# First expert's rows by products, its second matrix loaded earlier, routing's scratch moved, side projection spread over the experts

## What is computed

```python
# hier_moe, cut
g_gate, g_idx = top_k(softmax(xf @ w_rg), 1)            # one of 4 groups
e_w, e_i = top_k(softmax(e_logits of that group), 2)    # two of its 8 experts
hdn = silu(xb @ w1[e]) * (xb @ w3[e])                   # xb: the rows that chose expert e
out[rows] += (hdn @ w2[e]) * weight
# side projection, cut
h = h + rms_norm(p @ w_ple, g_ple) * sigmoid(rms_norm(h, g_plg) @ w_plg)
```

## Time and profile before

| | us |
|---|---|
| median of three runs | 1856.92 |
| lowest and highest of them | 1851.44, 1857.51 |
| the profiled execution's own time | 1853.95 |
| its span, first to last instruction | 1852.2 |

### The profile page before, as it was taken

One profiled execution on the slowest core, in us unless ns is written; L12 is line 12 of the kernel. 1 busy time (PEld: TensorE's weight loads), 2 busy tenths in 40 slices (PEclk: granted clock), 3 DMA queues, 4 the chain that ended last, 5 costly groups with the idle time before them and its releaser, 6 DMA issues. The chain is left out here.

```text
span 1852.2 us, 24687 instructions
## 1 busy us (share of the span) xinstructions
PE 1762.2 (95%) x9926; PEld 970.2 (52%) x9926; DVE 748.6 (40%) x1472; ACT 545.0 (29%) x1110; POOL 153.7 (8%) x194
## 2 busy tenths in 40 slices
PE   8999988989889899999899999999999999999998
PEld 3333455455444444555464444577645544566663
DVE  2244477142511121433223225577524328365642
ACT  2111477123101111333224112455412232344420
POOL 0310000001111110111100014000000003000000
PEclk9999999999999999999999999999999999999999
DMA  7664877448999999999970232000200012000001
GB/s 274 227 219 169 114 153 67 162 166 347 419 418 416 416 417 417 420 416 418 397 294 2 90 103 79 1 2 1 84 23 35 23 63 68 24 1 2 1 24 45
DMA packets 92194, 324.85 MB, mean 175 GB/s; under 512 B 12313, under 2 KB 28825, under 8 KB 65073
## 3 DMA queue, kind: packets, MB, share of 16 engines
q1 hardware_dynamic: 78224, 302.55, 45.1%
q10 hardware_dynamic: 8656, 12.32, 1.9%
q0 software_dynamic: 5200, 8.41, 1.2%
HBM read 317.58 MB, written 14.30 MB: 179 GB/s over the span
## 5 line engine op out<-in xcount | busy, mean ns | idle before, releaser
L1089 PE MATMUL mix_ps<-arena 128*64 128x256 f32 x2048 | 238.6, 386 | 9.1 <-DMA arena<-in_w 4.9
L2175 PE MATMUL tail_ps<-arena 128*128 128x512 f32 x504 | 220.1, 593 | 0.8 <-DMA arena<-in_w_plg 0.8
L1089 PEld LDWEIGHTS mix_ps<-arena 128*64 128x64 f32 x2048 | 145.3, 138 | 95.8 <-issue 23.7
L977 PE MATMUL mix_ps<-arena,side 128*128 128x512 f32 x384 | 174.1, 606 | 0.6 <-DMA arena<-in_w_in 0.6
L484 DVE TENSOR_REDUCE tail_small<-tail_ps 128x1 f32<-128x768 f32 x128 | 116.6, 953 | 123.4 <-PE tail_ps L351 77.5
L2175 PEld LDWEIGHTS tail_ps<-arena 128*128 128x128 f32 x504 | 95.0, 190 | 115.0 <-issue 114.5
L1101 PE MATMUL mix_ps<-arena 128*64 128x512 f32 x512 | 118.6, 606 | 22.1 <-DMA arena<-in_w 22.1
L977 PEld LDWEIGHTS mix_ps<-arena,side 128*128 128x128 f32 x384 | 71.8, 193 | 101.1 <-issue 82.9
L2175 PE MATMUL tail_ps<-arena,side 128*128 128x512 f32 (+2 forms) x320 | 119.6, 534 | 0.0
L575 ACT ACTIVATE arena<-tail_ps,tail_small 128x768 f32<-128x768 f32 x128 | 113.7, 898 | 3.7 <-DVE tail_small L484 3.7
L370 PE MATMUL tail_ps<-first,arena 128*128 128x128 f32 x768 | 98.5, 279 | 0.6 <-ACT arena L575 0.6
(11 more groups left out here) (392 smaller groups left out, 2339.5 us busy)
## 6 DMA issues: line engine op xcount, KB each, us to landing
arena<-in_w SPq DMA_DIRECT2D x96, 2048.0 KB, 21.2
arena<-in_l_w_mod SPq DMA_DIRECT2D x16, 1024.0 KB, 5.1
arena<-in_l_w_in SPq DMA_DIRECT2D x16, 1024.0 KB, 7.0
arena<-in_w_in SPq DMA_DIRECT2D x12, 1024.0 KB, 9.1
arena<-in_l_w_mod SPq DMA_DIRECT2D x16, 512.0 KB, 4.7
residual<-bias_blocks SPq DMA_DIRECT2D x32, 224.0 KB, 12.9
arena<-in_l_w_in ACTq DMA_DIRECT2D x12, 512.0 KB, 11.0
arena<-in_l_w_out SPq DMA_DIRECT2D x6, 1024.0 KB, 5.2
```

What stands on the lines that cost most here:

```text
L977: last = pe.matmul(ps[:, u % 4], oT[:, k, t * P:(t + 1) * P], weights.slot(W_IN[n, k // 4], 4, 512)[:, k % 4], start=(k == 0), stop=(k == ...
L1089: last = pe.matmul(out[h * CAP:(h + 1) * CAP, 0:H2], x, wb[:, k, h * H2:(h + 1) * H2], start=(k == 0), stop=(k == DK - 1))
L2175: last = pe.matmul(out, lhs(k), rhs(k), start=(k == 0), stop=(k == K - 1))
```

## The change

Four edits. (1) Routing's scratch leaves slot 4 for parts of `work` and `base`, and SyncE issues w2 of expert 0 ahead of its wait for `out_mm`, with no wait for `listed`. (2) Expert 0's rows are no longer gathered by DMA. VectorE makes `taken_0`, a 128x64 matrix for each row tile that has a row's factor `rs_h` in the column of its slot, TensorE multiplies it with `hx` (8 products into bank 1, `listed` = 1), and ScalarE copies the result to `xg[:, 0]`. `list_slots` comes behind the turning of these rows, GpSimd starts with `gather(1)`, and `listed` is 2 when the lists are done. (3) VectorE writes `index[:, 1]` and `gate_w` behind `take_x(0)` and `index[:, 0]`. (4) Side projection units 4 to 7 move into the experts: unit 4 behind expert 0's w3 product, units 5 to 7 behind `second(0)` in the loop's e = 1; their copies on ScalarE move too (unit 4 behind expert 0's Silu, 5 to 7 behind `outputs(0)`). SyncE's wait for `side_ev` = 8 stays where it was.

```diff
-    r_at = [2 * 4096]
+    r_in, r_at = (work[:, 4096:6144], base[:, late + CT * D:late + CT * D + 2592]), [0, 0]
...
+    taken_0, factor_0 = routing(XT, CAP), routing(XT)
...
+            expert(0, "w2")
             sp.wait_ge(s["out_mm"], 8)
             expert(1, "w1")
             expert(1, "w3")
-            sp.wait_ge(s["listed"], 1)
-            expert(0, "w2")
...
-            beside(2)
-
+            pe.wait_ge(s["hot"], 1)
+            for t in range(XT):
+                for h in range(2):
+                    last = pe.matmul(ps[h * CAP:(h + 1) * CAP, 1], taken_0[:, t], hx[:, t, h * 512:(h + 1) * 512], start=(t == 0), stop=(t == XT - 1))
+            last.then_inc(s["listed"], 1)
...
-            list_slots(4, hot, told, 3 * N_EXPERTS, s["hot"], s["listed"])
-            beside(3)
...
-            turn_rows(xg[:, 0], s["got"][0], 16, s["xg_turned"])
+            turn_rows(xg[:, 0], s["xn_done"], XT + 1, s["xg_turned"])
+            list_slots(4, hot, told, 3 * N_EXPERTS, s["hot"], 1, s["listed"])
...
+                if e == 0:
+                    beside(2, (0,))
...
                 if e == 1:
+                    beside(2, (1,))
+                    beside(3)
                     pe.wait_ge(s["side_ev"], 2 * XT)
...
+            for u in range(4):
+                beside(u)
+            act.wait_ge(s["listed"], 1)
+            act.activation(xg[:, 0], ps[:, 1], ACT.Copy).then_inc(s["xn_done"], 1)
...
+                if e == 0:
+                    beside(4)
...
+                if e == 1:
+                    for u in (5, 6, 7):
+                        beside(u)
...
+            dve.tensor_tensor(factor_0, A_all[:, :, 0], rs_h, ALU.mult)
+            dve.wait_ge(s["ranked"], 1)
+            chain(dve.tensor_tensor(taken_0, m["count"][:, 0:CAP].unsqueeze(1).to_broadcast([P, XT, CAP]),
+                                    ps[:, 4, 0:XT * N_EXPERTS].rearrange("p (t e) -> p t e", t=XT)[:, :, 0:1].to_broadcast([P, XT, CAP]), ALU.is_equal))
+            dve.tensor_tensor(taken_0, taken_0, factor_0.unsqueeze(2).to_broadcast([P, XT, CAP]), ALU.mult).then_inc(s["hot"], 1)
...
-            for e in range(2):
-                gather(e)
+
+            gather(1)
```

More of the change, by code:

```diff
@@ L690, in first_layer @@
     experts_over, trips_over, current = small_i[0:1, 100:100 + OVER + 1], small_i[0:1, 118:119], view(small_i, 120, 2)
-    r_at = [2 * 4096]
+    r_in, r_at = (work[:, 4096:6144], base[:, late + CT * D:late + CT * D + 2592]), [0, 0]
     def routing(*dims):
         n = math.prod(dims)
-        r_at[0] += n
-        assert r_at[0] <= 3 * 4096
-        return view(proj_w, r_at[0] - n, *dims)
+        z = 0 if r_at[0] + n <= 2048 else 1
+        r_at[z] += n
+        assert r_at[1] <= 2592
+        return view(r_in[z], r_at[z] - n, *dims)
     wr = routing(DK, N_GROUPS + N_EXPERTS)
@@ L1036, in _, with beside @@
             pe.wait_ge(s["side_in"], 16)
-            def beside(t):
-                for cc in range(2):
+            def beside(t, parts=(0, 1)):
+                for cc in parts:
                     u = 2 * t + cc
@@ L1052, in _, with list_slots @@
             pe.matmul(ps[:, 4, 256:256 + N_EXPERTS], m["ones"], A_sum[:, XT], start=True, stop=True).then_inc(s["ranked"], 1)
-            beside(2)
-            def list_slots(bank, lhs, rhs, n, done, listed):
+            pe.wait_ge(s["hot"], 1)
[3 more added lines that the diff above has]
+            last.then_inc(s["listed"], 1)
+            def list_slots(bank, lhs, rhs, n, done, done_0, listed):
                 for x in range(2):
-                    pe.wait_ge(done, x + 1)
+                    pe.wait_ge(done, done_0 + x + 1)
                     for t in range(XT):
@@ L1191, in _ @@
                 first_product(p3, matrix("w3", e)).then_inc(s["h3"], 1)
+                if e == 0:
+                    beside(2, (0,))
                 if e + 1 < STATIC:
-                    turn_rows(xg[:, 1 - p], s["got"][1 - p], 16 * ((e + 1) // 2 + 1), s["xg_turned"])
+                    turn_rows(xg[:, 1 - p], s["got"][1 - p], 16 * (e // 2 + 1), s["xg_turned"])
                 if e:
@@ L1215, in _ @@
                 if e == 6:
-                    list_slots(7, hot_2, told_2, 3 * OVER, s["over_hot"], s["listed"])
+                    list_slots(7, hot_2, told_2, 3 * OVER, s["over_hot"], 0, s["listed"])
             hidden(STATIC - 1)
@@ L1338, in _, with beside @@
             act.wait_ge(s["out_mm"], 2 * XT)
-            for u in range(2 * XT):
+            def beside(u):
                 act.wait_ge(s["side_mm"], u + 1)
                 act.activation(side[:, u * 512:(u + 1) * 512], ps[:, 5 + u % 3], ACT.Copy).then_inc(s["side_ev"], 1)
+            for u in range(4):
+                beside(u)
+            act.wait_ge(s["listed"], 1)
+            act.activation(xg[:, 0], ps[:, 1], ACT.Copy).then_inc(s["xn_done"], 1)
             def outputs(e):
@@ L1595, in _ @@
                     chain(dve.tensor_tensor(told[:, x, :, k], flat(O[:, x]), wide_row(told_of, N_EXPERTS), ALU.mult))
-            dve.wait_ge(s["ranked"], 1)
             for x in range(2):
@@ L1603, in _ @@
                                   rank[:, x].unsqueeze(2).to_broadcast([P, XT, 2 * CAP]), ALU.is_equal).then_inc(s["hot"], 1)
[L1605 to L1615, removed]
             def take_x(e):
@@ L1626, in gained_rows, with rows_to_write @@
                                          m["g_ffn_x"].rearrange("p (h j) -> p j h", h=2).unsqueeze(3).to_broadcast([P, 4, 2, CAP]), ALU.mult)
+            def rows_to_write(told_row, n, tmp, to):
+                chain(dve.scalar_tensor_tensor(out=tmp, in0=told_row, scalar=0.0, in1=m["twice_place"].to_broadcast([P, n]), op0=ALU.is_equal, op1=ALU.mult))
+                chain(dve.scalar_tensor_tensor(out=tmp, in0=told_row, scalar=m["spare_row"], in1=tmp, op0=ALU.add, op1=ALU.add))
+                return dve.tensor_copy(to, tmp)
+            take_x(0)
+            dve.wait_ge(s["listed"], 2)
+            chain(dve.tensor_tensor(slot_rows, ps[:, 4, 0:N_EXPERTS], m["spare_row"].to_broadcast([P, N_EXPERTS]), ALU.add))
+            dve.tensor_copy(index[:, 0], slot_rows).then_inc(s["indexed"], 1)
             def take_hidden(e):
@@ L1668, in overflow_listed @@
             def overflow_listed():
-                dve.wait_ge(s["listed"], 2)
+                dve.wait_ge(s["listed"], 3)
                 told_row = lambda k: ps[:, 7, k * OVER:(k + 1) * OVER]
@@ L1754, in context_step @@
                     dve.tensor_tensor(pr_c[:, u % 2], pr_c[:, u % 2], rc_c[:, u % 2].unsqueeze(2).to_broadcast([P, 2, CTX]), ALU.mult).then_inc(s["ctx_scaled"], 1)
-            take_x(0)
+            chain(dve.tensor_copy(gate_w, ps[:, 4, 2 * N_EXPERTS:3 * N_EXPERTS]))
+            chain(rows_to_write(ps[:, 4, N_EXPERTS:2 * N_EXPERTS], N_EXPERTS, slot_rows_2, index[:, 1]))
+            dve.sem_inc(s["indexed"], 1)
             for e in range(STATIC):
```

## The result

The changed kernel is slower: 1860.26 us against 1855.71 (medians of 12 runs each), ratio 1.0028 with a 95% interval of 1.0016 to 1.0041. A later round with 6 runs of the same kernel gave 1.0041 (1.0027 to 1.0054). On 1855 us that is +5.2 us (3.0 to 7.6) and +7.6 us (5.0 to 10.0). The forecast of +9.6 has the right sign and mechanism, and is too large.

A forecast was written before the change was run, and what follows sets the result against it. The prediction took the unbroken stream of expert weights as the bound: resuming 15.6 us later, less 5.0 and 1.0, gives +9.6 us, so 1863.5 from the profiled execution, 1866.5 from the median; forecast 1865 us, range 1858 to 1871.

The forecast's parts named there:

- The wait on `side_ev`: In SyncE's list: the wait holds g_ple and all later loads until about 439.1 us, a DMA pause of 20 us.
- The new chain to expert 0: From the counting products' end at 401.7 us, expert 0's w1 product starts near 410.0 at full clock.
- The chain from there to the eighth copy: On TensorE from expert 0's w1 product through side units 5 to 7: SyncE issues g_ple at about 439.1 us.
- The sum: Weight stream's end: 15.6 us later start, less 5.0 and 1.0 that no longer follow, net +9.6 us.
- 15.6 us later: Weight stream: it resumes at 439.1 instead of 423.5 us, when SyncE issues g_ple.
- 5.0 and 1.0: Taken off the stream: w1 of expert 2, 5.0 us, and three small indirect transfers falling in the pause, 1.0 us.
- The 9.4 MB behind the wait: Loads free to go at once behind SyncE's wait: g_ple, four matrices, context; 22.5 us, so no second pause.
- Rival 1: SyncE's wait does not hold the weight stream, only the earlier start counts: -8.5 us, 1845.5 us; chance 0.05.
- Rival 2: TensorE's slack from 736 us on absorbs the late stream, up to 9.6 us: 1854 to 1859 us; chance 0.10.
- Rival 3: Clock falls in the new chain and when TensorE waits at 446 us, 1.9 us each: 1867 to 1869; chance 0.15.
- w2 of expert 0, "nothing is won or lost": Its load moves from one DMA pause to another, issued at about 340 instead of 407.48 us: no gain or loss.

The follow-up runs named there:

- e1: Changed kernel with SyncE's wait for the eighth side copy and g_ple's load moved behind w3 of expert 3; 1844.0 us, ratio 0.9947 against the kernel before.
- e3: Kernel before with the fourth edit alone: side units 4 to 7 among the experts, SyncE's wait where it was; 1872.64 us, ratio 1.0096.
- e8: The changed kernel itself once more, for a second trace and more runs; ratio 1.0041 against the kernel before.
- e4: Kernel before with the first edit alone: scratch moved, w2 of expert 0 loaded early, no wait for `listed`; ratio 0.9973.
- e6: Changed kernel without its fourth edit: side units 4 to 7 ahead of the experts, SyncE's wait where it was; ratio 0.9979 against the kernel before.
- e5: The kernel of e3 with the wait for the eighth copy and g_ple's load moved behind w3 of expert 3; ratio 1.0006 against the kernel before.
- e7: Kernel before with the first and fourth edits, SyncE's wait and g_ple's load behind w3 of expert 3; ratio 0.9991.

## Why the prediction was right in kind and too large

**The wait on `side_ev`: right.** The whole sign of the result rested on one order row of SyncE's list. g_ple was issued at 436.85 us (forecast 439.1), the DMAs paused from 421 to 439, and e1, with nothing changed but the place of that wait and of the load behind it, is faster than the kernel before.

**The new chain to expert 0: right.** Forecast was expert 0's w1 product 8.3 us behind the end of the counting products; it starts 408.57 - 400.56 = 8.0 us behind it, at full clock, with gaps of 0.97 and 0.79 us.

**The chain from there to the eighth copy: a little too long.** I had SyncE's issue at 439.1 - 401.41 = 37.7 us behind the third counting product; it was 36.6 in both traces. Products in a series follow each other in 3.57 to 3.61 us rather than the 3.65 to 3.67 of a row by itself, whose end overlaps the start of the next: a merged row of 64 records takes 7.13 where I added 7.3. With the turnings, which overlap in the same way, that makes some 0.8 us from expert 0's w1 product on, and the 0.3 us of the shorter chain ahead of it comes on top.

**The sum: the form holds, a term was mis-sized.** The term is "15.6 us later", which was 36.6 - 22.1 = 14.5, too large by the 1.1 us of the paragraph above. With 5.0 and 1.0 taken off, that gives 8.5 us on the stream; the stage shows 7.9 and 7.3. The last 0.6 to 1.2 us are not explained. The prediction had the stream unbroken to the end of the experts, and it isn't: at 896 to 912 the DMA share is 0.92 before,

```profile
896.00:912.00 16.00, 15.41 (x108) 7.94 (x109) 2.39 (x5) 2.99 (x4) 2.02 (x2) 1.00 0.92 369
```

and 0.96 in the changed kernel at 902 to 918, so a late stream could find a little room there. But e1, whose stream is early, has 0.94 at 896 to 912, so lateness alone doesn't explain the difference, and it was not tested. In two places the working was off without harm. The 9.4 MB behind the wait took the context for 0.5 MB; it is 1024 KB, so it is 10.0 MB, and the stream is still unbroken (share 1.01 from 441 on). And TensorE's idle time between 480 and 734 did not grow with the delay (26.4 us before, 26.8 after): the delay shows as 7.6 idle us from 441 to 480, where the kernel before has 0.8 from 425.5 on.

**The whole time.** By the stage the change should be 7.3 to 7.9 us, by the product behind it 6.2 to 6.3; whole runs say 5.2 (3.0 to 7.6) and 7.6 (5.0 to 10.0). The first interval holds all of these but the 7.9 of the first trace, the second holds all. The prediction had no term for the 1.7 us that the kernel before loses to the clock in expert 30's w2 product. Why the two sets differ stays open; the clock's falls ahead of the stage (400 to 410 us at the third counting product) are one candidate.

**Rival 1, faster without the hold: the size was right, in part by luck.** Its -8.5 us was worked out for a wait that doesn't hold the stream. e1 makes that case and has -7.9 in the stage, -9.8 in whole runs. But the sum counted on a pause of 2.4 us ahead of w2 of expert 2, and e1 has none that the shares show:

```profile
448.50:480.00 31.50, 31.50 (x216) 16.64 (x216) 12.83 (x41) 12.62 (x20) 4.10 (x4) 1.00 1.01 417
```

Its release comes 10.0 us earlier than before and its stage ends 7.9 earlier; where the other 2.1 go stays open. The Trainium skill's rule ("DMA: Bandwidth & Descriptors", section "Anatomy of one DMA"), that the issuing sequencer waits and not the DMA engines, agrees with the 24.2 us in which SyncE issued nothing.

**Rival 2, absorbed: wrong.** e3 puts +19.8 us through to the end of the stage. TensorE's full stretch from 736 to 896 gives nothing back.

**Rival 3, the clock: wrong in its price.** In the new chain the clock did not fall. Of the two traces of the changed kernel the second fall is in one, e8: behind a wait of 2.27 us expert 2's w3 product took 5.27 us, where it took 3.67 in the first trace. Yet the stage of e8 is 0.6 us shorter, not 1.9 longer, since the stream sets the time there.

**w2 of expert 0, "nothing is won or lost": wrong.** The step overlooked what stood behind that load before: the first gather. Taking the 2 MB from ahead of it is worth 6.2 us of the stage (e4), more than the first three edits together gain in e6 (3.4). The loss to the clock that goes with the late gather was 9.21 - 7.13 = 2.1 us rather than 1.9. In the sum this did no harm, since the changed kernel has no first gather and its chain was added up anew; but part of the 10 us that I credited to the products was w2's.

## What to carry to other kernels

When work is moved later, look up every wait that names its semaphore, on the DMA-issuing engines first, and see what stands behind that wait: here a 0.5 MB load that nobody needed for 40 us (VectorE first uses it at 476.99 us) held 2 MB loads that everybody needed. In a stage that is bound by an unbroken stream of loads, time is set by when the stream starts and by its pauses (without a hold, from release to expert 30's w3 product took 496.3 to 498.5 us in six kernels), so the issuing engine's timeline and the DMA share by stretch tell more than the busy engine, which was 96% busy throughout the costly pause. And filling work that hides a wait is not free to move until the wait itself has gone.

## What the runs showed of the hardware

- A gather (some 0.14 MB) issued 1.4 us behind a 2 MB load was used 6.9 to 7.1 us after its issue (before, e3, e5), the same gather with the DMAs idle ahead of it after 3.6 and 3.7 (e4, e7). In the kernel before, packets of both queues ran side by side from 413 to 415 us, at a DMA share of about 1.0 and 398 to 422 GB/s, and none of the gather's ran ahead of 413.
- TensorE's clock after gaps: behind 4.9 us of idle time expert 0's 64 records took 9.21 us (partly at 1.2 GHz); behind 1.6 us and behind gaps of under 1 us they took 7.13 (2.4 GHz). In e7, e5 and e3 they took 9.42, 9.83 and 9.98 us, behind two gaps each (3.0 and 5.1, 3.7 and 8.6, 3.7 and 8.5 us), and the clock was down already in the products between the two. The length of one gap doesn't decide it: in two executions of the changed kernel expert 2's w3 product took 3.67 us behind a gap of 2.53 and 5.27 us behind one of 2.27.
- With the same instructions, the time at which one product starts some 400 us into the program varied from 400.25 to 409.99 us between executions (the changed kernel and e1), with PEclk 0.73 in the late one's last stretch though TensorE was busy all of it. Comparing single traces needs a landmark behind such places.
